# Attention heads of a two-layer decoder trunk: values as the stationary operand, probabilities normalised before their transposes

## What is computed

```
layer 0:  x += SGU mixer(norm(x));   x += SwiGLU(norm(x))
layer 1:  k = rms(norm(x) @ w_k), v = norm(x) @ w_v, q = rms(norm(x) @ w_q) / sqrt(128)    16 heads of 128
          o_h = softmax(causal(q_h k_h^T)) v_h
          x += o @ w_o;   x += SwiGLU(norm(x))
```

## Time and profile before

| | |
|---|---|
| median of 3 runs | 2162.88 us (2162.49 to 2166.7) |
| the profiled execution | 2162.54 us |
| its span, first to last instruction | 2160.8 us |
| TensorE's mean granted clock | 0.998 of full |
| PE busy | 2143.2 us (99%) |
| DVE busy | 1119.6 us (52%) |
| ACT busy | 998.3 us (46%) |
| DMA: moved, mean rate | 402.47 MB, 186 GB/s |

### The profile page before, as it was taken

The page is one execution under the profiler, slowest core; times in us unless marked ns, Lnnn a source line. Parts: engine busy times, 40 slices in busy tenths (PEclk is TensorE's granted clock), DMA queues, the critical chain, the costliest instruction groups (busy, mean ns, idle before and its releaser), DMA issues.

```text
span 2160.8 us, 25430 instructions
## 1 busy us (share of the span) xinstructions
PE 2143.2 (99%) x9774; PEld 1779.4 (82%) x9774; DVE 1119.6 (52%) x1222; ACT 998.3 (46%) x1229; POOL 30.3 (1%) x40
## 2 busy tenths in 40 slices
PE   8999999999999999999999999999999999999999
PEld 6888888888888888888888888788888888888887
DVE  4566554455545554444566566554555455544443
ACT  5444554444444444444566565454444444443332
POOL 0000000000000000000000000000000000000000
PEclk9999999999999999999999999999999999999999
DMA  7755555556555655554654544466555555555553
GB/s 247 240 175 175 180 191 186 186 192 194 180 189 193 194 179 193 193 195 149 222 193 159 170 167 148 156 195 195 187 185 191 191 186 188 193 188 192 192 192 131
DMA packets 201817, 402.47 MB, mean 186 GB/s; under 512 B 6592, under 2 KB 6688, under 8 KB 201504
## 3 DMA queue, kind: packets, MB, share of 16 engines
q1 hardware_dynamic: 200752, 398.49, 55.4%
q0 software_dynamic: 560, 3.15, 0.4%
q10 hardware_dynamic: 448, 0.04, 0.0%
HBM read 399.56 MB, written 2.10 MB: 186 GB/s over the span
## 4 chain that ended last, share of the span: by engine, by line
PE 98%; DVE 1%; ACT 0%; POOL 0%; issue 0%; DVEq 0%; ACTq 0%; POOLq 0%
PE acc L945 31%; PE acc L949 31%; PE acc L947 31%; PE tr L972 2%; PE tr L1035 0%; PE tr L1109 0%; PE tr L1099 0%; DVE w_lo L658 0%; PE tr L1117 0%; DVE a_lo L684 0%; ACT a_hi L383 0%; PE tr L1126 0%; PE tr L1127 0%; PE tr L1108 0%; PE tr L1125 0%
## 5 line engine op out<-in xcount | busy, mean ns | idle before, releaser
L658 DVE TENSOR_TENSOR w_lo<-raw,w_hi 128x1024 fp32r<-128x1024 f32 x656 | 803.0, 1228 | 859.9 <-ACT w_hi L349 859.3
L349 ACT ACTIVATE w_hi<-raw 128x1024 fp32r<-128x1024 f32 x656 | 692.7, 1060 | 928.5 <-PE acc L949 928.5
L945 PE MATMUL acc<-w_hi,a_hi 128*128 128x512 f32 x2048 | 806.1, 394 | 7.4 <-DVE w_lo L658 7.4
L949 PE MATMUL acc<-w_hi,a_lo 128*128 128x512 f32 x2048 | 799.1, 390 | 0.0
L947 PE MATMUL acc<-w_lo,a_hi 128*128 128x512 f32 x2048 | 798.1, 390 | 0.0
L945 PEld LDWEIGHTS acc<-w_hi,a_hi 128*128 128x128 f32 x2048 | 385.0, 188 | 87.5 <-issue 8.8
L949 PEld LDWEIGHTS acc<-w_hi,a_lo 128*128 128x128 f32 x2048 | 384.9, 188 | 80.9
L947 PEld LDWEIGHTS acc<-w_lo,a_hi 128*128 128x128 f32 x2048 | 385.3, 188 | 78.2
L945 PE MATMUL acc<-w_hi,h_hi 128*128 128x512 f32 x704 | 274.3, 390 | 0.0
L949 PE MATMUL acc<-w_hi,h_lo 128*128 128x512 f32 x704 | 273.9, 389 | 0.0
L947 PE MATMUL acc<-w_lo,h_hi 128*128 128x512 f32 x704 | 273.9, 389 | 0.0
(11 more groups left out here) (125 smaller groups left out, 785.0 us busy)
## 6 DMA issues: line engine op xcount, KB each, us to landing
raw<-in_ffn_w_gate_dram SPq DMA_DIRECT2D x88, 1024.0 KB, 5.1
raw<-in_ffn_w_up_dram SPq DMA_DIRECT2D x88, 1024.0 KB, 5.1
raw<-in_ffn_w_down_dram SPq DMA_DIRECT2D x88, 1024.0 KB, 4.9
raw<-in_a_w_in_dram SPq DMA_DIRECT2D x31, 1024.0 KB, 5.3
raw<-in_a_w_out_dram SPq DMA_DIRECT2D x16, 1024.0 KB, 4.9
raw<-in_w_v_dram SPq DMA_DIRECT2D x16, 1024.0 KB, 5.0
raw<-in_w_k_dram SPq DMA_DIRECT2D x16, 1024.0 KB, 4.9
raw<-in_b_w_q_dram SPq DMA_DIRECT2D x16, 1024.0 KB, 4.9
```

The source lines that it names most:

```text
L349: nc.scalar.activation(dst, src, ACT.Copy).then_inc(hi_split, 1)
L658: nc.vector.tensor_tensor(lo, src, hi, ALU.subtract).then_inc(lo_split, 1)
L945: nc.tensor.matmul(acc[s][t][:, :], hi[:, kb, tok], w_hi[:, slot, k, :], start=kb == 0, stop=False)
L949: ins = nc.tensor.matmul(acc[s][t][:, :], lo[:, kb, tok], w_hi[:, slot, k, :], start=False, stop=kb == HG * n - 1)
```

## The change

- `transpose_probs` waits for a new step of DVE, `scale_probs`, in place of the exponentials: reciprocal of the row sums, then the probabilities times it, in place in `prob` (one operation of 128 columns, one of 256). It is DVE's hook 12 + 3h, behind its split of that half-group (in `wo`: 7 + 2h).
- `values` makes v the stationary operand and the transposed probabilities the moving one: one product of 256 columns and one of 128, and o comes out with the head's dimensions on partitions, as the projection wants it.
- ACT copies it per head to `o_hi`, DVE writes `o_lo` per head (256 columns each), at hook 14 + 3h (in `wo`: 8 + 2h). The staging of o and its 8 transposes per block are gone, and so are their batch numbers and waits.
- `maxima` and `exps` keep their places (11 + 3h; in `wo` 6 + 2h); they now stand behind `o_lo` and `o_hi` of the head before.
- PE's loop over `qkv_body` is a Python loop, so that the program has its three bodies one after the other; those of ACT and DVE stay loops.

```diff
--- before.py
+++ after.py
@@ -73,8 +73,8 @@
         for g in range(units * kb // (2 * HG)):
             slots[g % per_body % RAW] += 1
 
-    batches = {"x": 0, "gated": NC, "x1": 2 * NC, "h0": 3 * NC, "x2": 3 * NC + NF, "o": 4 * NC + NF,
-               "x3": 5 * NC + NF, "h1": 6 * NC + NF, "out": 6 * NC + 2 * NF}
+    batches = {"x": 0, "gated": NC, "x1": 2 * NC, "h0": 3 * NC, "x2": 3 * NC + NF, "x3": 4 * NC + NF,
+               "h1": 5 * NC + NF, "out": 5 * NC + 2 * NF}
 
 
     WO_FIRST = [(0, 0), (0, 1), (0, 2), (1, 0), (1, 1), (1, 2), (0, 3), (1, 3)]
@@ -198,7 +198,8 @@
         kq_raw, kq_squared, kq_ss, kq_rs = sem("kq_raw"), sem("kq_squared"), sem("kq_ss"), sem("kq_rs")
         kq_normed, kq_transposed, kq_ready = sem("kq_normed"), sem("kq_transposed"), sem("kq_ready")
         scored, maxed, exped = sem("scored"), sem("maxed"), sem("exped")
-        probT_done, probT_ready, pv_done, head_out = sem("probT_done"), sem("probT_ready"), sem("pv_done"), sem("head_out")
+        probT_done, probT_ready, pv_done, prob_scaled = sem("probT_done"), sem("probT_ready"), sem("pv_done"), sem("prob_scaled")
+        o_hi_ready, o_lo_ready = sem("o_hi_ready"), sem("o_lo_ready")
         pool_step, act_step, dve_step = sem("pool_step"), sem("act_step"), sem("dve_step")
         stored = sem("stored")
 
@@ -591,16 +592,17 @@
                 nc.scalar.activation(probT[:, :, :].rearrange("p n s -> p (n s)"), tr[1][:, 0:3 * P], ACT.Copy)\
                     .then_inc(probT_ready, 1)
 
-            def o_hi_part(i):
-                lhs_hi_part(i + batches["o"], o_hi, i * HPC)
+            def o_hi_part(i, h):
+                act.wait_ge(pv_done, i * HPC + (h + 1))
+                dst = o_hi[:, bass.ds(i * HPC + h, 1), :].rearrange("p k s -> p (k s)")
+                nc.scalar.activation(dst, tr[1][:, 0:S], ACT.Copy).then_inc(o_hi_ready, 1)
 
             def attention_hooks(i):
 
                 hooks = {7: [lambda: take_kqT(i, 0)], 9: [lambda: take_kqT(i, 1)]}
                 for h in range(HPC):
-                    for off, f in ((0, exps), (2, take_probT)):
-                        hooks.setdefault(min(11 + 3 * h + off, 23), []).append(lambda h=h, f=f: f(i, h))
-                hooks.setdefault(23, []).append(lambda: o_hi_part(i))
+                    for off, f in ((0, exps), (2, take_probT), (3, o_hi_part)):
+                        hooks.setdefault(11 + 3 * h + off, []).append(lambda h=h, f=f: f(i, h))
                 return hooks
 
             def qkv_body(i, first):
@@ -625,9 +627,8 @@
             g = NC - 1
             hooks = {2: [lambda: read_kq(g, 1)], 4: [lambda: take_kqT(g, 0)], 5: [lambda: take_kqT(g, 1)]}
             for h in range(HPC):
-                hooks[6 + 2 * h] = [lambda h=h: exps(g, h)]
-                hooks[7 + 2 * h] = [lambda h=h: take_probT(g, h)]
-            hooks[14] = [lambda: o_hi_part(g)]
+                for off, f in ((0, exps), (1, take_probT), (2, o_hi_part)):
+                    hooks.setdefault(6 + 2 * h + off, []).append(lambda h=h, f=f: f(g, h))
             unit(hg_before["wo"], [16 * (slot_n[n % RAW] + n // RAW + 1) for n in range(len(WO_FIRST))], hooks, n=16)
 
             def x3(c):
@@ -862,30 +863,28 @@
                                                   AX_X, ALU.max, negate=True)
                 ins.then_inc(maxed, 1)
 
-            def head_output(i, h):
+            def scale_probs(i, h):
 
                 dve.wait_ge(exped, i * HPC + (h + 1))
                 step.inc(nc.vector.reciprocal(row_inv[:, :], row_sum[:, :]))
                 step.wait()
-                dve.wait_ge(pv_done, i * HPC + (h + 1))
-                if h == 0:
-                    dve.wait_ge(transposed, i + batches["o"])
-                    dve.wait_ge(res_saved, 2 * NC)
-                for t in range(TT):
-                    ins = nc.vector.tensor_scalar(stage[:, t, h * P:(h + 1) * P], tr[1][:, t * P:(t + 1) * P],
-                                                  row_inv[:, t:t + 1], None, ALU.mult)
-                ins.then_inc(staged if h == HPC - 1 else head_out, 1)
-
-            def o_lo_part(i):
-                lhs_lo_part(i + batches["o"], o_hi, o_lo, i * HPC)
+                for t, (a, b) in enumerate(((0, 1), (1, 3))):
+                    part = prob[:, a:b, :].rearrange("p n s -> p (n s)")
+                    ins = nc.vector.tensor_scalar(part, part, row_inv[:, t:t + 1], None, ALU.mult)
+                ins.then_inc(prob_scaled, 1)
+
+            def o_lo_part(i, h):
+                dve.wait_ge(o_hi_ready, i * HPC + (h + 1))
+                row = bass.ds(i * HPC + h, 1)
+                nc.vector.tensor_tensor(o_lo[:, row, :].rearrange("p k s -> p (k s)"), tr[1][:, 0:S],
+                                        o_hi[:, row, :].rearrange("p k s -> p (k s)").bitcast(F32), ALU.subtract)\
+                    .then_inc(o_lo_ready, 1)
 
             def attention_hooks(i):
-                hooks = {4: [lambda: square_sums(i, 1)], 6: [lambda: norm_heads(i, 1)], 11: [lambda: maxima(i, 0)]}
+                hooks = {4: [lambda: square_sums(i, 1)], 6: [lambda: norm_heads(i, 1)]}
                 for h in range(HPC):
-                    hooks[14 + 3 * h] = [lambda h=h: head_output(i, h)]
-                    if h < HPC - 1:
-                        hooks[14 + 3 * h].append(lambda h=h: maxima(i, h + 1))
-                hooks[23].append(lambda: o_lo_part(i))
+                    for off, f in ((0, maxima), (1, scale_probs), (3, o_lo_part)):
+                        hooks.setdefault(11 + 3 * h + off, []).append(lambda h=h, f=f: f(i, h))
                 return hooks
 
             def qkv_body(i, first):
@@ -911,9 +910,8 @@
             g = NC - 1
             hooks = {3: [lambda: square_sums(g, 1)], 4: [lambda: norm_heads(g, 1)]}
             for h in range(HPC):
-                hooks.setdefault(6 + 2 * h, []).append(lambda h=h: maxima(g, h))
-                hooks[8 + 2 * h] = [lambda h=h: head_output(g, h)]
-            hooks[14].append(lambda: o_lo_part(g))
+                for off, f in ((0, maxima), (1, scale_probs), (2, o_lo_part)):
+                    hooks.setdefault(6 + 2 * h + off, []).append(lambda h=h, f=f: f(g, h))
             unit(hg_before["wo"], hooks, n=16)
 
             def x3(c):
@@ -1088,9 +1086,9 @@
             def transpose_heads(i, n):
 
                 pe.wait_ge(kq_normed, i * 2 + (n + 1))
-                if n == 0:
-                    pe.wait_ge(lhs_lo, i + batches["o"])
-                else:
+                if n == 0 and not (isinstance(i, int) and i == 0):
+                    pe.wait_ge(o_lo_ready, i * HPC)
+                elif n == 1:
                     pe.wait_ge(kq_ready, i * 2 + 1)
                 nat = (k_nat, q_nat)[n]
                 for h in range(HPC):
@@ -1110,9 +1108,9 @@
                                  start=True, stop=True).then_inc(scored, 1)
 
             def transpose_probs(i, h):
-                pe.wait_ge(exped, i * HPC + (h + 1))
+                pe.wait_ge(prob_scaled, i * HPC + (h + 1))
                 if h:
-                    pe.wait_ge(head_out, i * (HPC - 1) + h)
+                    pe.wait_ge(o_lo_ready, i * HPC + h)
                 for n in range(3):
                     ins = nc.tensor.transpose(tr[1][:, n * P:(n + 1) * P], prob[:, n, :], ident[:, :])
                 ins.then_inc(probT_done, 1)
@@ -1121,10 +1119,10 @@
                 pe.wait_ge(probT_ready, i * HPC + (h + 1))
                 if h == 0:
                     pe.wait_ge(val_ready, i + 1)
-                v = [val[:, t, bass.ds(i * CH + h * P, P)] for t in range(TT)]
-                nc.tensor.matmul(tr[1][:, 0:P], probT[:, 0, :], v[0], start=True, stop=True)
-                nc.tensor.matmul(tr[1][:, P:2 * P], probT[:, 1, :], v[0], start=True, stop=False)
-                nc.tensor.matmul(tr[1][:, P:2 * P], probT[:, 2, :], v[1], start=False, stop=True).then_inc(pv_done, 1)
+                v = [val[:, t, i * CH + h * P:i * CH + (h + 1) * P] for t in range(TT)]
+                nc.tensor.matmul(tr[1][:, 0:2 * P], v[0], probT[:, 0:2, :].rearrange("p n s -> p (n s)"),
+                                 start=True, stop=False)
+                nc.tensor.matmul(tr[1][:, P:2 * P], v[1], probT[:, 2, :], start=False, stop=True).then_inc(pv_done, 1)
 
             def attention_hooks(i):
                 hooks = {3: [lambda: transpose_heads(i, 0)], 5: [lambda: transpose_heads(i, 1)]}
@@ -1132,14 +1130,13 @@
                     hooks.setdefault(7 + 3 * h, []).append(lambda h=h: scores(i, h))
                     hooks[9 + 3 * h] = [lambda h=h: transpose_probs(i, h)]
                     hooks[10 + 3 * h] = [lambda h=h: values(i, h)]
-                hooks[21] = [lambda: transpose_batch(i + batches["o"])]
                 return hooks
 
             base = hg_before["qkv"]
 
             def qkv_body(i, hooks, lhs_waits):
                 for n in range(3):
-                    if not isinstance(i, int):
```

(8 more changed lines are left out.)

## The result

| | before | after |
|---|---|---|
| median (5 runs each) | 2162.88 us | 2208.13 us (2205.15 to 2212.96) |
| ratio of the two, 95% interval | | 1.0206 [1.0194, 1.0217] |
| the profiled execution, its span | 2162.54, 2160.8 us | 2205.15, 2203.3 us |
| mean granted clock, profiled execution | 0.998 | 0.992 |
| mean granted clock of the five runs | | 0.992, 0.990, 0.988, 0.990, 0.990 |

The change makes the kernel slower by 45 us. The page of the changed kernel: span, busy time of the engines (beside the earlier trace rows), shares of the chain that ended last.

The account below looks back on a forecast made before the run. PE, busy for 99% of the span, was taken to bound the kernel. 2162.54 us plus 39.4 of new waits less 5.9 of gains gave 2196, plus 18 for the lower clock 2214 us; range 2193 to 2224.

Parts of the forecast that it names:

- Both its mechanisms: Attention: PE waits in each of 16 heads, and its clock falls to half behind 12 of these waits.
- The place of the scaling: DVE scales only after ACT's and DVE's next splits, so PE's transposes wait in each of 16 heads.
- Size of the waits: PE delays: 27.3 us over three loop blocks (2.5 or 2.2 per head), 12.1 us in the output projection; 39.4 together.
- The gains: PE saves 2.6 us of o transposes in the loop and 3.3 us in the output projection, 5.9 us together.
- Waits and gains: Whole kernel at full PE clock: 39.4 us of delays less 5.9 saved, 33.5 us net, giving 2196 us.
- The clock: Slow stretches at half clock behind 12 of the 16 new PE waits, 1.5 us each, 18 us, giving 2214 us.
- The Trainium skill's rule: PE's clock drops behind idle gaps over about 3 us; none here is that long, so nothing drops.
- That the clock holds: Rival: PE's 16 new waits come but its clock stays up; 2196 us, 2191 with the cheapest scaling; chance 0.22.
- That the scaling hides: Rival: DVE scales at once after the exponentials, before PE's transposes, leaving only the savings; 2156.6 us; chance 0.03.
- Follow-on waits for `w_lo`: Rival: PE, once late, waits again for `w_lo` in each head, 21 us on top; 2235 us; chance 0.08.

Follow-up runs that it names:

- five products in the wait: Changed kernel with five idle 128-column PE products put ahead of each head's wait for the scaled probabilities; 2194.80 us, ratio 1.0139 to the kernel before.
- scaling ahead of the split: Changed kernel with `scale_probs` moved ahead of DVE's next split, right behind `maxima`; 2159.08 us, ratio 0.9979 to the kernel before.
- without the scaling: Changed kernel with the division by the row sums left out, transposes waiting for the exponentials, so attention is not computed; 2156.47 us, ratio 0.9963 to the kernel before.
- scaling moved in the kernel before: Kernel before with probabilities scaled behind DVE's next split; o still staged and transposed, copied instead of scaled; 2218.90 us, ratio 1.0253.
- loop written out, kernel before: Kernel before with only PE's loop over the blocks written out three times; 2165.34 us, ratio 1.0009.
- two products in the wait: Changed kernel with two idle 128-column PE products ahead of each head's wait for the scaled probabilities; 2196.73 us, ratio 1.0153 to the kernel before.
- five products behind the wait: Changed kernel with five idle 128-column PE products after each head's waits for the scaled probabilities and `o_lo`; 2222.23 us, ratio 1.0276 to the kernel before.
- scaling one more place back: Changed kernel with the loop's scaling moved behind DVE's split of half-group 13 + 3h, output projection unchanged; 2223.19 us, ratio 1.0285 to the kernel before.

## Why the prediction was right

The forecast was 2214 us in a range of 2193 to 2224; measured are 2208. Both its mechanisms are there. The waits were seen without the drops (2194.8), and where the waits were taken away the drops were gone from the attention too (2159.1 and 2156.5). Term by term:

- **The place of the scaling** decided it. Moving it ahead of one split takes about 50 us away, moving it back by one in the loop adds 15, and it does its harm in the old layout too.
- **Size of the waits.** 39.4 us were forecast as delays. Measured by starts: head 0 of a block 1128.06 - 1119.55 = 8.51 us from scores to transposes, where it was 6.13 (scores at 1121.07 in the profile before), so 2.4 late (2.5 forecast); heads 1 and 2 8.84 (1140.04 - 1131.20) against 6.82, so 2.0 (2.2); in the output projection head 0 6.00 (1376.60 - 1370.60) against 3.41 (scores at 1336.68 before), 2.6 (2.8), the others 6.74 (1386.48 - 1379.74) against 4.10, 2.6 (3.1). With three blocks: 3 x (2.4 + 3 x 2.0) + 2.6 + 3 x 2.6 = 35.6 us. The term that was too big is the scaling: 0.65 taken, 0.55 as records and 0.47 until DVE is free. As PE's list has them the waits are 33.6 us, the longest 2.5, where the prediction wanted 34 to 38 and 2.9: just below, by the same term. The estimate from the Trainium skill's table ("VectorE: DVE Perf Modes", the perf-mode tier table) was 0.5; its 1.23 us for 2048 columns make at most 0.08 us for 128 of them, an estimate from the page; 128 more columns cost 0.348 - 0.287 = 0.06 us here, so the trace agrees. The copy to `o_hi` was 0.36 instead of 0.45, `o_lo` as forecast.
- **The gains.** From the last `values` to the next half-group 1412.46 - 1410.71 = 1.75 us against 5.20 (1.87 forecast). Together 2.6 + 3.4 = 6.0 us.
- **Waits and gains** give 35.6 - 6.0 = 29.6, so 2162.5 + 29.6 = 2192 us; with the clock kept up in the attention 2194.8 were measured (five products in the wait; its profiled execution has two more drops at the start of the kernel than the one before).
- **The clock.** What remains of the median is 2208.1 - 2192 = 16 us. In a block without a drop heads follow each other at 12.0 us (1140.04, 1152.04 above). In the last block of the loop they don't:

```profile
1299.82 0.56 PE L1115 MATMUL tr<-ident,prob 128*128 128x128 f32 x3 [2.23 <-DVE prob L873]
...
1313.39 0.55 PE L1115 MATMUL tr<-ident,prob 128*128 128x128 f32 x3 [1.89 <-DVE prob L873]
...
1326.94 0.55 PE L1115 MATMUL tr<-ident,prob 128*128 128x128 f32 x3 [1.88 <-DVE prob L873]
...
1340.51 0.55 PE L1115 MATMUL tr<-ident,prob 128*128 128x128 f32 x3 [1.88 <-DVE prob L873]
```

  These are 13.57, 13.55 and 13.57 us: 1.55 us per drop, 1.5 forecast. The profiled execution has nine drops in the attention, 9 x 1.55 = 14 us, and at the start of the kernel one where the profile before has two, so 2192 + 14 - 1.5 = 2204.5; measured are 2205.15. The median lies 3 us higher and has a lower mean clock (0.990 against 0.992, which is 9 us more at the lower level, or 4 us of time). The five executions order themselves by their clock, from 2205.15 at 0.992 to 2212.96 at 0.988. Forecast were 12 drops at 1.5 us, 18 us, against the 16 that remain. The number was a guess between one half and all, and the reason given for it did not hold: that the new waits are "all longer than the four" at the start is true of seven, while the other nine are of 1.84 to 1.90 us where those four are of 1.80 to 1.96; and longer waits brought no more drops. Right was that drops come and what one costs; that 12 is near is luck in part.
- **The Trainium skill's rule** ("TensorE: Matmul & The Clock Gate", "Why this matters for your kernels"), no drop without idle gaps of over about 3 us, would have given 2196 us. The runs differ from it: in the attention drops stand behind gaps of 1.88 us, and at the start of the kernel behind gaps of 1.81 to 1.85. With gaps of at most 1.4 us (the five products) there were none in the attention.
- **The rivals.** That the clock holds was wrong; near its 2196 us is only the kernel with products in the waits. That the scaling hides was wrong for the order that the change wrote, and right for the other: with two lines changed the kernel is at 2159, not the 2157 of that rival, for four short waits in the output projection, which the rival had overlooked. Follow-on waits for `w_lo` did not come.

**How far one profile's count carries.** Every kernel here begins alike, with four waits of PE for `w_lo` of 1.6 to 2.0 us in the first 41 us. Drops in the profiled executions, read in windows of 2 us:

| kernel | at the 4 waits at the start | at the 12 waits of the loop | at the 4 of the output projection |
|---|---|---|---|
| before | 2 | no such waits | no such waits |
| changed | 1 | 8 | 1 |
| scaling ahead of the split | 0 | no such waits | 0 (waits of 0.4 us) |
| without the scaling | 2 | no such waits | no such waits |
| scaling moved in the kernel before | 3 | 9 | 1 |
| five products in the wait | 4 | 0 | 0 |
| loop written out, kernel before | 0 | no such waits | no such waits |
| two products in the wait | 2 | 0 | 2 |
| five products behind the wait | 0 | 3 | 2 |
| scaling one more place back | 1 | 3 | 2 |

(Two more stand at the old 2.5 us wait for `o_lo`: one where the scaling moved in the kernel before, and the long one of the loop written out.) The waits at the start have 15 drops out of 40, from none to all four in one execution. So how many of a kernel's waits are followed by a drop changes from one execution to the next, and the difference between eight and three in the loop may be no more than that. The scatter of the runs goes with the clock too: the 34 runs of the kernel before go from 2159.61 us at a mean clock of 1.000 to 2169.01 at 0.995.

**What stays open**: which of the waits bring a drop. Their length doesn't tell: waits of 1.8 us at the start had drops, 12 of 1.43 to 1.79 us in the loop had none (the two products), and 12 of 3.5 us had three. And the gap at the end of the attention left the clock alone in one execution and not in another. The drops of the last block come in a row, at heads that follow each other 13.56 us apart; whether one drop brings the next, by where in time it puts the next wait, no run here tests.

## What to carry to other kernels

In a program whose order is written out by hand, a new step costs not its own time but that of everything which stands between its input and it: 0.5 us of scaling cost 2.0 to 2.6 per head, since a split of two engines stood in between. Put right behind its input it cost nothing in the loop and 0.4 us per head in the output projection. Ask of each added step when its input is there, and what its engine has to do first. And where the main engine is full, count the idle time twice: as time, and for what it does to the clock; a few otherwise useless matmuls in a wait that can't be avoided gave 13 us back here.

## What the runs showed that had not been expected

- The same four waits at the start of the kernel were followed by anything from no drop to four, 15 in 40. The count in one profile says little about a kernel; the mean clocks of all its runs say more.
- Waits of PE of 3.5 us brought no more drops than waits of 1.9 to 2.2 us, and in the latter the drops came in rows, at all four heads of the last block.
- Idle times of up to 1.8 us in the loop left the clock alone throughout in the profiled execution (two products in the wait), two of the four of about 2 us behind it did not, and neither did two of 1.8 us at its start.
- Two operations of DVE on 128 and 256 columns between buffers take 0.29 and 0.35 us: doubling the columns adds 0.06.
